# Latent norms of an MLA layer: sums in four column strips, one 260-column reciprocal and root, spread by one-row products

## The reference

```python
def mla_project(h, pos, w_in, q_norm_w, kv_norm_w, w_uq):
    cq, ckv, kr = jnp.split(h @ w_in, [Q_LORA, Q_LORA + KV_LORA], axis=-1)   # 512, 256, 32
    q = (rms_norm(cq, q_norm_w) @ w_uq).reshape(b, L, MLA_HEADS, QK_NOPE + QK_ROPE)
    q_nope = q[..., :QK_NOPE]
    q_rope = rope(q[..., QK_NOPE:], pos)
    ckv = rms_norm(ckv, kv_norm_w)
    kr = rope(kr[:, :, None, :], pos)[:, :, 0, :]
    ...
def rms_norm(x, w):
    y = xf * lax.rsqrt(jnp.mean(xf * xf, axis=-1, keepdims=True) + RMS_EPS)
    return (y * w)
```

## Time and profile before

| | us |
|---|---|
| median of three runs | 2341.1 (2340.46 to 2343.3) |
| profiled execution | 2342.06 |
| its span, first to last instruction | 2340.4 |
| PE busy | 2281.7 (97%) |
| DVE / ACT / POOL busy | 1135.0 / 787.5 / 190.1 |
| mean granted TensorE clock | 0.992 |

### The profile page before, as it was taken

The page is one execution under the profiler, slowest core; times in us unless marked ns, Lnnn a source line. Parts: engine busy times, 40 slices in busy tenths (PEclk is TensorE's granted clock), DMA queues, the critical chain, the costliest instruction groups (busy, mean ns, idle before and its releaser), DMA issues.

```text
span 2340.4 us, 49135 instructions
## 1 busy us (share of the span) xinstructions
PE 2281.7 (97%) x19694; PEld 2213.9 (95%) x19694; DVE 1135.0 (48%) x1776; ACT 787.5 (34%) x1395; POOL 190.1 (8%) x247
## 2 busy tenths in 40 slices
PE   7999999998999999999999999999999999999998
PEld 7999999898878999999999999999997789999997
DVE  4444333676545644444334444433666755444433
ACT  4332233454334433332333233333224334322222
POOL 1000001013100010000010000001213511000000
PEclk9999999999999999999999999999999999999999
DMA  3333333223233333333333323333445823333333
GB/s 125 91 93 91 98 103 110 70 79 111 89 121 132 90 87 87 93 90 94 103 94 101 90 90 90 99 100 95 139 167 187 282 96 94 90 95 97 91 104 105
DMA packets 119618, 249.46 MB, mean 107 GB/s; under 512 B 15232, under 2 KB 15376, under 8 KB 118144
## 3 DMA queue, kind: packets, MB, share of 16 engines
q1 hardware_dynamic: 105552, 193.05, 28.1%
q0 software_dynamic: 13792, 54.43, 6.8%
q10 hardware_dynamic: 144, 0.09, 0.0%
HBM read 237.30 MB, written 9.95 MB: 106 GB/s over the span
## 4 chain that ended last, share of the span: by engine, by line
PE 71%; DVE 3%; ACT 0%; issue 0%; DVEq 0%; ACTq 0%
PE psum L353 61%; PE psum L2232 2%; PE psum L2277 1%; PE psum L2269 1%; PE psum L1110 1%; DVE w_low L331 1%; PE psum L2201 1%; PE psum L2175 1%; PE psum L2325 1%; PE psum L2219 0%; PE psum L1097 0%; DVE keys L2538 0%; PE psum L1034 0%; PE psum L2180 0%; PE psum L1113 0%
## 5 line engine op out<-in xcount | busy, mean ns | idle before, releaser
L331 DVE TENSOR_TENSOR w_low<-w_raw,w_high 128x512 fp32r<-128x512 f32 x718 | 518.8, 741 | 646.2 <-ACT w_high L325 645.7
L353 PE MATMUL psum<-x_high,w_high 128*128 128x260 f32 x3840 | 775.4, 283 | 14.4 <-DVE w_low L331 10.5
L353 PE MATMUL psum<-x_low,w_high 128*128 128x260 f32 x3840 | 772.3, 283 | 0.0
L353 PE MATMUL psum<-x_high,w_low 128*128 128x260 f32 x3840 | 770.7, 282 | 0.0
L353 PEld LDWEIGHTS psum<-x_high,w_high 128*128 128x128 f32 x3840 | 590.4, 189 | 19.3 <-DMA constants<-in_constants_dram 6.6
L353 PEld LDWEIGHTS psum<-x_low,w_high 128*128 128x128 f32 x3840 | 593.6, 189 | 0.0
L353 PEld LDWEIGHTS psum<-x_high,w_low 128*128 128x128 f32 x3840 | 592.5, 189 | 0.0
L325 ACT ACTIVATE w_high<-w_raw 128x512 fp32r<-128x512 f32 x718 | 433.2, 623 | 452.3 <-PE psum L353 435.2
L353 PE MATMUL psum<-hidden_high,w_low 128*128 128x260 f32 x1408 | 283.9, 283 | 0.0
L353 PE MATMUL psum<-hidden_low,w_high 128*128 128x260 f32 x1408 | 282.9, 282 | 0.0
L353 PE MATMUL psum<-hidden_high,w_high 128*128 128x260 f32 x1408 | 282.9, 282 | 0.0
(11 more groups left out here) (374 smaller groups left out, 1760.0 us busy)
## 6 DMA issues: line engine op xcount, KB each, us to landing
w_raw<-in_weights_dram SPq DMA_DIRECT2D x720, 256.0 KB, 2.7
cache_pages<-in_cache_pages_dram POOLq DMA_DIRECT2D x128, 272.0 KB, 4.1
ret_sample_state<-in_state_ret_dram POOLq DMA_DIRECT2D x2, 2048.0 KB, 7.6
out_ret_s_dram<-ret_sample_state POOLq DMA_DIRECT2D x2, 2048.0 KB, 7.6
out_y_dram<-residual SPq DMA_DIRECT2D x8, 260.0 KB, 2.2
ssm_sample_state<-in_state_ssm_dram POOLq DMA_DIRECT2D x2, 1024.0 KB, 5.4
out_ssm_s_dram<-ssm_sample_state POOLq DMA_DIRECT2D x2, 1024.0 KB, 4.7
residual<-in_x_dram SPq DMA_DIRECT2D x3, 520.0 KB, 6.9
```

The source lines that it names most:

```text
L331: nc.vector.tensor_tensor(WL[:, slot, :], WRAW[:, slot, :], WH[:, slot, :].bitcast(F32), ALU.subtract).then_inc(w_split, 1)
L353: mm = nc.tensor.matmul(PS[:, b0 + 2 * m + half, 0:cols], w, x[:, half * cols:(half + 1) * cols], start=start, stop=stop)
```

## The change

The sums of each norm and half go into a strip of 32 columns of the array, so that partitions 0 to 31 and 32 to 63 hold the query's two halves and 64 to 127 those of kv, all in one bank. V2 shrinks to 260 columns: two scalar operations on 64 partitions each, one reciprocal and one root then serve both norms. PE waits for the root at k = 2 of uq 0 (`lr_done`), after the first of its two weight chunks, and spreads the four rows by one-row products into the four banks of "mla cnorm". DVE, after the reciprocal, waits for that spread (`lspread_full`), makes TAB and scales the kv latents straight from PSUM, and gives the banks of "mla cnorm" back only then; it drains uq 0 and uq 1 after that. ACT has one root and four splits in a row. The buffer R2 is gone.

```diff
--- before.py
+++ after.py
@@ -2019,7 +2019,7 @@
     KRX = at("rotary_parts", [P, T], REGION + 41600)
     KRB = at("rotary_second", [P, T], REGION + 43680)
     TABK = at("key_table", [P, T], REGION + 45760)
-    V2 = at("latent_variance", [P, 2, T], REGION + 47840)
+    V2 = at("latent_variance", [P, 2, TH], REGION + 47840)
     CKH = at("kv_latent_high", [P, 2, T], REGION + 53824, F32R)
     CKL = at("kv_latent_low", [P, 2, T], REGION + 57984, F32R)
     PT = at("probs_by_key", [P, 1280], REGION + 53824)
@@ -2044,7 +2044,6 @@
     PB = [at(f"probs{i}", [P, 1280], ZONE + 5120 * i) for i in range(2)]
     SQC = at("latent_squares", [P, 6, T], GU_OFF)
     KRT = at("rotary_key", [P, T], ZONE + 24960)
-    R2 = at("latent_rstd", [P, 2, T], e.SQT_OFF)
     small = [ZONE + 27648]
 
     def little(name, shape):
@@ -2071,6 +2070,7 @@
     loaded, wuk_loaded, wuv_loaded = sem("mla_tables_loaded"), sem("w_uk_loaded"), sem("w_uv_loaded")
     page_loaded = [sem(f"cache_pages_loaded{i}") for i in range(3)]
     lsq_done, xqh_done, xq_done = sem("latent_squares_done"), sem("q_high_done"), sem("q_low_done")
+    lspread_full = sem("latent_rstd_spread")
     lv_done, lr_done = sem("latent_rcp_done"), sem("latent_rstd_done")
     ckn_done, ckh_done, ck_done = sem("kv_normed_done"), sem("kv_high_done"), sem("kv_low_done")
     kr_done, krr_done = sem("rotary_key_done"), sem("keys_rotary_done")
@@ -2114,15 +2114,27 @@
         acquire(pe, step)
         pe.wait_ge(lsq_done, 3)
         b = bank0(step)
-        for which, tiles in enumerate((range(4), range(4, 6))):
-            for half in range(2):
-                for t in tiles:
-                    mm = nc.tensor.matmul(PS[:, b + 2 * which + half, 0:TH], ONES, SQC[:, t, half * TH:(half + 1) * TH],
-                                          start=t == tiles[0], stop=t == tiles[-1])
+        for n in range(4):
+            for q in range(4 if n < 2 else 2):
+                t = n + 4 * (q // 2)
+                mm = nc.tensor.matmul(PS[32 * q:32 * q + 32, b, 0:TH], ONES[:, 0:32], SQC[:, t, (q % 2) * TH:(q % 2 + 1) * TH],
+                                      start=n == 0, stop=n == (1 if q >= 2 else 3))
         mm.then_inc(full(step), 1)
+
+        def latent_spread(k):
+            pe.wait_ge(xq_done, k + 1)
+            if k != 2:
+                return
+            pe.wait_ge(lr_done, 1)
+            b = bank0("mla cnorm")
+            for q in range(4):
+                mm = nc.tensor.matmul(PS[:, b + q, 0:TH], ONES[32 * q:32 * q + 1, :], V2[32 * q:32 * q + 1, 1, :],
+                                      start=True, stop=True)
+            mm.then_inc(lspread_full, 1)
+
         for g in range(8):
             e.gemm(pe, ("uq", g), 2, 4, lambda k: (XQH[:, k, :], XQL[:, k, :]),
-                   before_k=(lambda k: pe.wait_ge(xq_done, k + 1)) if g == 0 else None)
+                   before_k=latent_spread if g == 0 else None)
         step = "smp qlat"
         acquire(pe, step)
         wait_free(pe, ("uq", 7))
@@ -2350,11 +2362,8 @@
         a.splits(2)
         a.splits(2)
         act.wait_ge(lv_done, 1)
-        nc.scalar.activation(R2[:, 0], V2[:, 0], ACT.Sqrt).then_inc(lr_done, 1)
-        a.splits(2)
-        act.wait_ge(lv_done, 2)
-        nc.scalar.activation(R2[:, 1], V2[:, 1], ACT.Sqrt).then_inc(lr_done, 1)
-        a.splits(2)
+        nc.scalar.activation(V2[:, 1], V2[:, 0], ACT.Sqrt).then_inc(lr_done, 1)
+        a.splits(4)
         act.wait_ge(ckn_done, 2)
         for t in range(2):
             nc.scalar.activation(CKH[:, t, :], CKF[:, t, :], ACT.Copy).then_inc(ckh_done, 1)
@@ -2497,20 +2506,19 @@
         step = "mla cnorm"
         wait_full(dve, step)
         b = bank0(step)
-        nc.vector.tensor_scalar(halves(V2[:, 0, :]), PS[:, b:b + 2, 0:TH], 1.0 / QL, EPS, ALU.mult, ALU.add)
-        nc.vector.tensor_scalar(halves(V2[:, 1, :]), PS[:, b + 2:b + 4, 0:TH], 1.0 / KVL, EPS, ALU.mult,
-                                ALU.add).then_inc(free(step), 1)
-        wait_free(dve, step)
-        nc.vector.reciprocal(V2[:, 0], V2[:, 0]).then_inc(lv_done, 1)
-        dve.wait_ge(lr_done, 1)
-        link(nc.vector.tensor_tensor(TAB[:], TABR[:], R2[:, 0, :], ALU.mult))
+        nc.vector.tensor_scalar(V2[0:64, 1], PS[0:64, b, 0:TH], 1.0 / QL, EPS, ALU.mult, ALU.add)
+        link(nc.vector.tensor_scalar(V2[64:128, 1], PS[64:128, b, 0:TH], 1.0 / KVL, EPS, ALU.mult, ALU.add))
+        nc.vector.reciprocal(V2[:, 0], V2[:, 1]).then_inc(lv_done, 1)
+        dve.wait_ge(lspread_full, 1)
+        nc.vector.tensor_tensor(halves(TAB[:]), halves(TABR[:]), PS[:, b:b + 2, 0:TH], ALU.mult)
+        for t in range(2):
+            ins = nc.vector.scalar_tensor_tensor(halves(CKF[:, t, :]), halves(CKF[:, t, :]), PV[:, V_KVNORM + t:V_KVNORM + t + 1],
+                                                 PS[:, b + 2:b + 4, 0:TH], ALU.mult, ALU.mult)
+            ins.then_inc(ckn_done, 1)
+        dve.wait_ge(ckn_done, 2)
+        dve.sem_inc(free("mla cnorm"), 1)
         uq(0)
-        nc.vector.reciprocal(V2[:, 1], V2[:, 1]).then_inc(lv_done, 1)
         uq(1)
-        dve.wait_ge(lr_done, 2)
-        for t in range(2):
-            nc.vector.scalar_tensor_tensor(CKF[:, t, :], CKF[:, t, :], PV[:, V_KVNORM + t:V_KVNORM + t + 1], R2[:, 1, :],
-                                           ALU.mult, ALU.mult).then_inc(ckn_done, 1)
         for t in range(2):
             dve.wait_ge(ckh_done, t + 1)
             nc.vector.tensor_tensor(CKL[:, t, :], CKF[:, t, :], CKH[:, t, :].bitcast(F32), ALU.subtract).then_inc(ck_done, 1)
```

## The result

The changed kernel takes 2351.0 us (median of 6 runs, 2348.3 to 2354.2) against 2341.5 us before (6 runs): a ratio of 1.0038, 95% interval 1.0028 to 1.0048. It is slower by 9.5 us where 6.3 was forecast, and 0.8 us above the upper end of the range. The profiled execution took 2354.19 us, with a span of 2352.5 us, 12.1 us longer than that of before. Two of all the executions behind this document, both in later sets, took 2791.7 and 3727.6 us at mean granted clocks of 0.749 and 0.556; medians and ratios leave them out.

What follows compares the result with a forecast made beforehand. The TensorE, busy 97% of the span, was taken as the bound. A 4.2 us later uq 2 plus 2.1 us of low clock gave +6.3 us: 2347.4 us against the median of 2341.1, range 2344.8 to 2350.2.

Steps and rivals of the forecast that it cites:

- DVE held until the copy ends: Before the norm chain, a weight split beside GpSimd's 7.08 us keys copy keeps VectorE from the sums until 1683.78.
- Strips worth nothing: Sums before uq 0 take 1.9 instead of 5.07 us, but the 3.2 us saved turn into TensorE idle time.
- The chain by the line between 130 and 520 columns: Norm chain at 260 columns, interpolated: 3.1 us, so TensorE goes on at 1686.9 after 9.3 us idle at k = 2.
- The spread and the late release: Inside uq 0: spreading adds 0.65 us; sums' banks return at 1689.7, hidden 0.7 us before uq 0 ends.
- Full-clock loss of 4.2 us: uq 2 starts at 1696.2 against 1692.01, 4.2 us late, and that loss stays from uq 3 on.
- The clock, 2.1 us: Behind the 9.3 us idle stretch in uq 0, low clock adds 2.1 us, at 0.45 us lost per us.
- two cases of 5.6 and 3.8 us: Work until full clock returned after two earlier idle stretches of 8.20 and 3.79 us; they give 2.5 and 1.7 us lost.
- the upper bound of 2.5: Low-clock loss behind the idle stretch by the long case: 2.5 us, against 1.7 by the short one.
- Runs of one kernel lie within 2.8 us of each other: Whole-kernel run spread of 2.8 us, used with the chain, spread and clock bounds for the forecast's own range.
- The rival that DVE is not held: VectorE free at 1676.9 before the chain, idle time 2.4 us, uq 2 at 1689.3: -2.7 us, 2338.4 us; chance 5%.

Runs made afterwards that it cites:

- the second profile: The changed kernel run again with no edit, with its own profile: 2348.6 us (7 runs), ratio 1.0029 to the kernel before.
- the kernel with all of it together: Changed kernel with keys copy in 8 pieces, wait at k = 3, norm chain ahead of the splits, one split during the root: 2336.0 us, ratio 0.9983.

## Why the prediction was right and wrong

- *DVE held until the copy ends*: right. The chain began at 1686.79, 10.94 us after the sums began (forecast 1683.78 - 1672.73 = 11.05). That the copy is the cause rested, before the experiments, on its times alone (7.08 us over a split of 7.52 us that ended 0.55 us behind it); with the copy in pieces the two splits took 2.14 instead of 8.12 us.
- *Strips worth nothing*: right. They take 1.9 us, and three times as much leaves the start of uq 2 where it was (25.42 against 25.46).
- *The chain by the line between 130 and 520 columns*: right. 0.42, 0.43, 1.78 and 0.42 us, 9.19 us idle (9.3). From 1686.79 to the end of the wait at 1690.07 it took 3.28 us (3.1): the second scalar operation began 0.44 us after the first, behind its end, and not 0.34.
- *The spread and the late release*: the spread took 1.17 us from 1690.07 to the next product, at low clock, which the term of 0.65 left to the clock term. At full clock it takes 0.65, as forecast (1679.06 to 1679.71 in the kernel with all of it together). The banks were free at 1693.41, before uq 0 was over (1695.55).
- *Full-clock loss of 4.2 us*: right, 4.3 with the gap filled.
- *The clock, 2.1 us*: right in kind. Its price of 0.45 us is worked out from the earlier trace rows: 23 products in 5.00 us at a granted clock of 0.50 (0.217 us each), against 0.12 us each at 1.00. Its two cases of 5.6 and 3.8 us run from the end of each idle stretch of the earlier trace rows to the end of the low clock (28.28 to 33.90, 463.63 to 467.39). The changed kernel shows the same pace: two products start every 0.43 us at low clock (1692.28 to 1692.71) and every 0.24 us behind it (1694.59 to 1694.83). The low clock cost 1.9 us in one profile (4.1 us of work at low clock), 2.6 in the other (5.7 us), so the upper bound of 2.5 was just too narrow.
- *Runs of one kernel lie within 2.8 us of each other*: this is the step that failed. It rested on three runs, and the forecast put nothing into its sum for the clock in phases that the change doesn't touch. The changed kernel's 13 runs span 2347.3 to 2354.2, 6.9 us, and 23 runs of the kernel before span 2341.0 to 2351.0. In the profile the untouched parts cost 3.1 us ahead of the sums and 2.8 us behind uq 2, which the second profile doesn't have. In the first six runs of the changed kernel three happened to be of the upper kind (2353.5 to 2354.2) and three of the lower (2348.3 to 2348.6), so that the median fell in the empty middle, at 2351.0. The median of all 13 is 2348.6. In the second set the change cost 6.6 us, near the forecast of 6.3; the interval there runs from 4.0 to 9.6 us, so the whole kernel's time alone would not bear out the sum to this accuracy. The stretch does: +6.2 and +6.9. The mechanism was right; what was mis-sized is how much low clock in other phases adds to a run, which the trace of before could have suggested: its mean granted clock of 0.992 already holds stretches at 0.50 behind short waits, as at 1730 behind 1.45 us.
- *The rival that DVE is not held* was priced at -2.7 us. Made true by the pieces it gave -0.1 in the stretch: the idle time was 3.22 and not 2.4 us, and idle time below the two stretches of the earlier trace rows was taken to cost no clock. In that profile it did, with 3.4 us at 0.50 behind it.

What stays open: why an execution has more or fewer stretches at low clock in the untouched phases. Waits of 1.44 and 1.45 us at the same place had low clock behind them in one execution and none in another; the runs don't show what decides.

## What to carry to other kernels

A shorter chain on an engine gains nothing while that engine is held by something ahead of the chain: ask first when the chain can start, and look beside it for a GpSimd copy over an unusually long VectorE instruction (here 7.07 us of copy, and a split of 7.5 instead of 0.7 us). A wait moved into the middle of a gemm can turn into idle time of the TensorE plus slower work behind it (here 9.19 us, and 4.1 to 5.7 us of work at a granted clock of 0.50), and the second part doesn't appear among the waits. Where clock stretches make single runs differ by more than the change, compare one stretch of the trace, from a common start, before believing a median, and don't put the low clock of one profile down to one short wait.

## What the runs showed of the hardware

- One split of 0.69 us took 7.5 us beside one whole copy and 1.5 us beside pieces of 1.05 us (median); the scale table's product took 1.49 us with both inputs in SBUF beside a piece (kernel before in pieces), 0.70 with one of them in PSUM. The reciprocal (1.78 us), the scalar operations (0.42 and 0.43) and the scale table's product by a PSUM operand (0.70) took as long beside the whole copy as after it.

```profile
1686.72 1.49 DVE L2506 TENSOR_TENSOR query_scale<-rope_table,latent_rstd 128x520 f32<-128x520 f32 x1 [0.70 <-ACT latent_rstd L2353]
```

- Idle stretches of 9.19, 3.22 and 1.78 us of the TensorE were each followed by work at 0.50 of the clock (5.7 or 4.1, about 3.4 and 3.4 us); one of 1.04 us followed by one of 1.14 was not.
- Twelve float32 products in strips of 32 columns, in sets of 4, 4, 2 and 2, took 1.87 us (changed kernel, 1675.85 to 1677.72) against 5.07 in full width.
- Every float32 product named here left two records, which the forecast calls passes: the 12 of the sums 24, three times as many 72, the 21 in the filled gap 42, the four of the spread 8. The 32 records of the earlier trace rows are of 16 products, so that its 0.24 us is for four records. The 48 products of a uq group, of rounded parts, left 48.
